# A hybrid decoder layer: a shorter chain per threshold search round, key searches over halves of 128, and the sampled u/v product moved into the front end

## What is computed

```python
z = x @ w_in                        # q, k, v, qi, ki, wi, u, vb, ga, gb
# token mixer A: a light indexer scores every visible key, each query keeps 256
sc = einsum(relu(einsum(qi, ki)), wi) * scale
_, idx = lax.top_k(sc, 256)
attn = softmax over the kept keys
# token mixer B: gMLP on chunks of 128
vn = layer_norm(vb); gm = u * (w_spatial @ vn + b_spatial)
# merge
ga, gb = sigmoid(ga + bias_a), sigmoid(gb + bias_b)
merged = ga * (attn @ w_branch_a) + gb * (gm @ w_branch_b)
h = layer_norm(alpha * x + merged @ w_o)      # then a mixture of 32 experts
```

## Time and profile before

| | us |
|---|---|
| median of 3 runs | 1486.02 (1482.46 to 1490.97) |
| the profiled execution | 1475.57 |
| its span, first to last instruction | 1474.1 |
| PE busy in the span | 1357.8 (92%) |
| DVE busy | 719.0 (49%) |
| ACT, POOL busy | 281.8, 240.7 |
| L906 (counts of the search), busy | 174.2 and 77.0 |
| `choose_keys_and_gate`, PE's first to last instruction | 291.3 to 718.4 |

### The profile page before, as it was taken

How to read it: one execution, slowest core, us unless ns; L and a number is a source line. 1 busy time by engine, 2 the same in 40 slices (tenths; PEclk the granted TensorE clock), 3 DMA queues, 4 the chain that set the end, 5 groups by cost and what they waited for, 6 DMA issues and landing times. The chain is left out here.

```text
span 1474.1 us, 19420 instructions
## 1 busy us (share of the span) xinstructions
PE 1357.8 (92%) x6779; PEld 699.5 (47%) x6779; DVE 719.0 (49%) x1687; ACT 281.8 (19%) x624; POOL 240.7 (16%) x292
## 2 busy tenths in 40 slices
PE   7999999699999999989899989899963999999986
PEld 2444444244456666656577746455541333333321
DVE  0200123488888888995365953456671111111135
ACT  0100112222231111110266420000000111111124
POOL 3121000033230000020135100001111111111103
...
GB/s 320 81 58 48 16 16 72 89 48 1 0 98 69 65 65 68 71 65 20 52 88 116 59 76 360 264 29 29 29 29 246 331 404 406 404 414 409 404 158 233
DMA packets 70330, 214.03 MB, mean 145 GB/s; under 512 B 16459, under 2 KB 42059, under 8 KB 59882
## 3 DMA queue, kind: packets, MB, share of 16 engines
...
## 5 line engine op out<-in xcount | busy, mean ns | idle before, releaser
L906 DVE TENSOR_SCALAR_CACHE_REDUCE front<-score,bound 128x384 bf16<-128x384 f32 (+2 forms) x198 | 174.2, 942 | 19.2 <-DVE bound L932 18.9
L234 PE MATMUL ps_front<-front,x_all 128*128 128x512 f32 (+1 forms) x448 | 180.4, 557 | 1.7 <-ACT wi L364 1.7
L1819 PE MATMUL main_ps_experts<-w_gate_up,main_e_rowsT 128*32 128x512 f32 (+1 forms) x1280 | 172.6, 603 | 1.6 <-DVE main_e_rowsT L1927 1.6
L234 PEld LDWEIGHTS ps_front<-front,x_all 128*128 128x128 f32 x448 | 83.2, 190 | 91.7 <-issue 81.2
L1528 PE MATMUL ps_merge<-w_o,mergedT 128*128 128x512 f32 x256 | 114.9, 608 | 3.0 <-DVE h_rows L1667 3.0
L733 PE MATMUL ps_gate<-x_all,w_gate 128*128 128x344 f32 x384 | 116.0, 461 | 0.0
L733 PE MATMUL ps_gate<-x_all,front 128*128 128x344 f32 x384 | 113.2, 453 | 0.0
L1819 PEld LDWEIGHTS main_ps_experts<-w_gate_up,main_e_rowsT 128*32 128x32 f32 (+1 forms) x1280 | 50.4, 117 | 106.6 <-issue 106.6
L1932 DVE TENSOR_TENSOR main_hidden<-main_hidden,main_ps_experts 128x256 f32<-128x256 f32 x24 | 10.1, 421 | 174.6 <-ACT main_hidden L1879 174.6
L733 PEld LDWEIGHTS ps_gate<-x_all,w_gate 128*128 128x128 f32 x384 | 74.3, 194 | 38.9 <-issue 2.4
L733 PEld LDWEIGHTS ps_gate<-x_all,front 128*128 128x128 f32 x384 | 72.7, 190 | 37.5
(11 more groups left out here) (304 smaller groups left out, 1712.5 us busy)
## 6 DMA issues: line engine op xcount, KB each, us to landing
...
w_gate_up<-pair_out SPq DMA_DIRECT2D x8, 1024.0 KB, 14.0
...
h_rows<-in_x_rows SPq DMA_DIRECT2D x9, 512.0 KB, 6.0
...
```

The costliest lines, as they stand in the source:

```text
L234: mm = nc.tensor.matmul(ps[:, g % 2, 0:c1 - c0], x_all[:, k, t * P:(t + 1) * P], w[:, k, c0:c1], start=(k == 0), stop=(k == KC - 1))
L906: V.tensor_scalar(waste[0:n, at - width:at], s, column(bound, g), None, compare, ALU.add, accum_out=column(number, g)).then_inc(taken, 1)
L1819: mm = nc.tensor.matmul(ps[c0:c1, GU, :], rowsT[j][:, k, c0:c1], w_gu[b][:, k, :], start=(k == 0), stop=(k == KC - 1))
```

## The change

- **Search.** A table of 31 powers of two (and a zero) is loaded into `bits`, the first DMA of the stage. In round r the step `other` (the bound with the next round's bit set as well, an exclusive or with column r+1 of the table) is made before the counts; after them `missed` says which rows counted too few, and `bound` becomes `other`, with the bit of column r taken back where it was missed. `found_bits`, `reached` and `bit` are gone, and with them two of the four chained steps. The two columns are addressed by the loop's register.
- **Sampled u/v product.** It moves into the front end as `make_few_uv`, four blocks of weights behind the matmuls of unit 10 and four behind those of unit 11, into bank 0. Both stages use one PSUM tensor. ACT waits for it at the end of the front end.
- **Banks for u.** u alternates between banks 6 and 0; PE waits for the copy of two tiles back. One more wait stands before tile 1 (bank 0 read) and before the first gate product in bank 6.
- **Key searches.** The one-hots are over 128 ranks, in four buffers of half the size: a place over 128 is reduced by 128 (`upper`), and the page numbers and places are split by half into four columns (`ids_by_half`, two new steps). PE does 16 matmuls with four columns per sample, ahead of single products from `at` = 3 on, and turns the places one product later.
- **Gates.** In piece 5 the products come in the order 1, 2, 0; the stores in the order merged_b, gate_a, with one more wait before gate_a in piece 5.
- **End.** The wait for the landing of the stores moves from the end of the stage to the start of `attend` on SP, POOL and DVE.

```diff
+            def make_few_uv(ks):
+                for k in ks:
+                    if k == 0:
+                        pe.wait_ge(early_in, 16 * KC // 2)
+                        pe.wait_ge(acc_read, AFTER_FEW + 5 * (NT - 1) + 4)
+                    if k >= KC // 2:
+                        pe.wait_ge(w_uv_in[k], 16)
+                    for g in range(4):
+                        mm = nc.tensor.matmul(ps[g * FEW:g * FEW + N_SAMPLE, FEW_UV_BANK, 0:QUARTER], x_few[:, k, 0:N_SAMPLE],
+                                              w_uv(k)[:, g * QUARTER:(g + 1) * QUARTER], start=(k == 0), stop=(k == KC - 1))
+                if ks[-1] == KC - 1:
+                    mm.then_inc(few_uv_full, 1)
...
             for n in range(len(units) - 2, len(units)):
                 score_dots(n)
+                make_few_uv(range(0, KC // 2) if n < len(units) - 1 else range(KC // 2, KC))
...
-        U, V, MIX, TURN = 0, 1, 2, 3
-        FEW_BANK, FEW_SQUARES, FEW, QUARTER = 4, 5, 32, GW // 2
+        ps = keep["ps_mixer"]
+        U, V, MIX, TURN = (6, FEW_UV_BANK), 1, 2, 3
...
+        def products(at):
+            return (1, 2, 0) if at == 5 else (0, 1, 2)
...
+            sp.dma_start(bits[:], ins["bits"].to_broadcast([P, 32])).then_inc(bits_in, 16)
...
-                    for which, name in ((0, "gate_a"), (1, "merged_b")):
+                    for which, name in ((1, "merged_b"), (0, "gate_a")):
+                        if at == 5 and which == 0:
+                            sp.wait_ge(gates_read, (blk - j) * 9 + at * 3 + 9)
...
-            def make_few():
-                for k in range(KC):
-                    if k >= KC // 2:
-                        pe.wait_ge(w_uv_in[k], 16)
-                    for g in range(4):
-                        mm = nc.tensor.matmul(ps[g * FEW:g * FEW + N_SAMPLE, FEW_BANK, 0:QUARTER], x_all[:, k, SEQ:SEQ + N_SAMPLE],
-                                              w_uv(k)[:, g * QUARTER:(g + 1) * QUARTER], start=(k == 0), stop=(k == KC - 1))
-                mm.then_inc(uv_full, 1)
...
             def make_uv(t):
-                for b in (U, V):
-                    if t >= 1:
-                        pe.wait_ge(uv_read, 2 * t - 1 + b)
+                if t == 1:
+                    pe.wait_ge(few_step, 4)
+                if t >= 2:
+                    pe.wait_ge(uv_read, 2 * t - 3)
+                for half, bank in enumerate((U[t % 2], V)):
+                    if half and t >= 1:
+                        pe.wait_ge(uv_read, 2 * t)
                     for k in range(KC):
-                        mm = nc.tensor.matmul(ps[:, b, :], x_all[:, k, t * P:(t + 1) * P], w_uv(k)[:, b * GW:(b + 1) * GW],
+                        mm = nc.tensor.matmul(ps[:, bank, :], x_all[:, k, t * P:(t + 1) * P], w_uv(k)[:, half * GW:(half + 1) * GW],
                                               start=(k == 0), stop=(k == KC - 1))
                     mm.then_inc(uv_full, 1)
...
                 if (at, which) == (0, 2):
                     turn(LAST - 1)
                     mix(LAST)
+                    pe.wait_ge(uv_read, 2 * NT - 2)
...
-                        for which in range(3):
+                        for which in products(at):
                             if ahead:
                                 ahead(at, which)
-                            pe.wait_ge(gates_read, i * 18 + at * 3 + which + 1)
+                            pe.wait_ge(gates_read, i * 18 + at * 3 + products((at + 4) % 6).index(which) + 1)
...
+            seek_at = {(3, 0): 0, (3, 1): 1, (3, 2): 2, (4, 0): 3, (4, 1): 4, (4, 2): 5, (5, 1): 6, (5, 2): 7}
+
+            def find_rows(at, which):
+                if (at, which) == (2, 1):
                     turn_places()
-                for b in ((), (), (0, 1), (2, 3), (4, 5), (6, 7))[at]:
+                if (at, which) in seek_at:
+                    b = seek_at[at, which]
                     pe.wait_ge(hot_ready, b + 1)
-                    for half in range(2):
-                        for g in range(PAGES):
-                            mm = nc.tensor.matmul(ps[:, TURN, b * 4 + half * 2:b * 4 + half * 2 + 2],
-                                                  hot[b % 2][:, g, half * P:(half + 1) * P],
-                                                  ids[:, b, g, :], start=(g == 0), stop=(g == PAGES - 1))
+                    for g in range(PAGES):
+                        mm = nc.tensor.matmul(ps[:, TURN, b * 4:b * 4 + 4], hot[b % HOTS][:, g, :],
+                                              ids_by_half[:, b, g, :, :].rearrange("p half c -> p (half c)"),
+                                              start=(g == 0), stop=(g == PAGES - 1))
                     mm.then_inc(hot_used, 1)
 
-            make_gates(KC // 2 - 1, between=find_rows)
+            make_gates(KC // 2 - 1, ahead=find_rows)
...
-            for tile in (bound, number, found_bits):
-                step(V.memset(tile[:], 0), wait=False)
-            step(V.memset(bit[:], 1 << 30))
+            for tile in (bound, number):
+                step(V.memset(tile[:], 0), wait=(tile is number))
             count_all(ALU.is_ge)
             step.n += N_SEARCH
             dve.wait_ge(taken, step.n)
             step(V.tensor_scalar(flip[:], number[:], float(TOPK), -1.0, ALU.is_lt, ALU.mult))
-            step(V.scalar_tensor_tensor(bound[:].bitcast(I32), found_bits[:], bit[:], flip[:],
-                                        ALU.bitwise_or, ALU.bitwise_xor))
-            per_round = N_SEARCH + 4
+            dve.wait_ge(bits_in, 16)
+            step(V.tensor_scalar(bound[:].bitcast(I32), flip[:], bits[:, 0:1], None, ALU.bitwise_xor))
+            per_round = N_SEARCH + 3
             with dve.Fori(0, 31) as r:
                 done = r * per_round + step.n
+                V.tensor_scalar(other[:], bound[:].bitcast(I32), bits[:, bass.ds(r + 1, 1)], None,
+                                ALU.bitwise_xor).then_inc(taken, 1)
                 count_all(ALU.is_ge)
-                wait_alone(dve, taken, done + N_SEARCH, idle[0])
-                V.tensor_scalar(reached[:], number[:], float(TOPK), -1.0, ALU.is_ge, ALU.mult).then_inc(taken, 1)
                 wait_alone(dve, taken, done + (N_SEARCH + 1), idle[0])
-                V.scalar_tensor_tensor(found_bits[:], reached[:], bit[:], found_bits[:],
-                                       ALU.bitwise_and, ALU.bitwise_or).then_inc(taken, 1)
+                V.tensor_scalar(missed[:], number[:], float(TOPK), -1.0, ALU.is_lt, ALU.mult).then_inc(taken, 1)
                 wait_alone(dve, taken, done + (N_SEARCH + 2), idle[0])
-                V.tensor_scalar(bit[:], bit[:], 1, None, ALU.logical_shift_right).then_inc(taken, 1)
+                V.scalar_tensor_tensor(bound[:].bitcast(I32), missed[:], bits[:, bass.ds(r, 1)], other[:],
+                                       ALU.bitwise_and, ALU.bitwise_xor).then_inc(taken, 1)
                 wait_alone(dve, taken, done + (N_SEARCH + 3), idle[0])
-                V.scalar_tensor_tensor(bound[:].bitcast(I32), found_bits[:], bit[:], flip[:],
-                                       ALU.bitwise_or, ALU.bitwise_xor).then_inc(taken, 1)
-                wait_alone(dve, taken, done + (N_SEARCH + 4), idle[0])
             step.n += 31 * per_round
...
-            step(nc.vector.tensor_copy(place[:], ps[:, MIX, 0:P].rearrange("p (g b) -> p g b", b=N_SAMPLE)))
+            turned = ps[:, MIX, 0:P].rearrange("p (g b) -> p g b", b=N_SAMPLE)
+            step(nc.vector.tensor_scalar(upper[:], turned, float(P), None, ALU.is_gt))
+            step(nc.vector.scalar_tensor_tensor(place[:], upper[:], -float(P), turned, ALU.mult, ALU.add), wait=False)
+            step(nc.vector.tensor_tensor(ids_by_half[:, :, :, 1, :], ids[:],
+                                         upper[:].rearrange("p g b -> p b g").unsqueeze(3).to_broadcast([P, N_SAMPLE, PAGES, 2]),
+                                         ALU.mult))
+            step(nc.vector.tensor_tensor(ids_by_half[:, :, :, 0, :], ids[:], ids_by_half[:, :, :, 1, :], ALU.subtract))
             step(nc.vector.tensor_copy(keep["own_taken"][:], ps[0:1, MIX, 256:256 + N_SAMPLE]))
-            dve.sem_inc(hot_used, 2)
-            with dve.Fori(0, N_SAMPLE // 2) as i:
-                for j in range(2):
-                    b = i * 2 + j
+            dve.sem_inc(hot_used, HOTS)
+            with dve.Fori(0, N_SAMPLE // HOTS) as i:
+                for j in range(HOTS):
+                    b = i * HOTS + j
                     dve.wait_ge(hot_used, b + 1)
                     for g in range(PAGES):
                         last = nc.vector.tensor_scalar(hot[j][:, g, :], rank_b[:], place[:, g, bass.ds(b, 1)], None,
                                                        ALU.is_equal)
                     last.then_inc(hot_ready, 1)
-            dve.wait_ge(hot_used, N_SAMPLE + 2)
+            dve.wait_ge(hot_used, N_SAMPLE + HOTS)
...
+        def wait_for_gates_stored(eng):
```

(6 more changed lines are left out.)

58 lines of the change are left out of this document (29 added, 29 removed).

## The result

The changed kernel takes **1466.9 us** (median of 4 runs, 1464.5 to 1468.2) against 1488.5 us for the kernel before in the same rounds. The ratio is 0.985, 95% interval 0.983 to 0.987. In two later series, on two chips, the medians were 1454.2 against 1476.5 us (ratio 0.987, 0.984 to 0.990) and 1469.1 against 1489.7 us (0.987, 0.984 to 0.990). So the change takes off 20.6 to 22.3 us in all three; on which chip the first measurement ran isn't on record. The forecast of 1462.3 us was 4.6 us too low and its range, 1455 to 1474, held the time.

What follows compares the result with a forecast made beforehand. It took the rebuilt stage as PE-bound, a faster DVE worth only PE's waits for it. A to E sum to 23.7 us: profile 1475.57 to 1451.9, median 1486.02 to 1462.3 us; range 1455 to 1474 (8 in 10).

Steps and rivals of the forecast that it cites:

- A: Front end's end: sampled product moved into PE's idle time, score matmuls faster, less a slow start; 6.0 us gained.
- B: gMLP tiles: with u in alternate banks, six PE waits for ScalarE's copy of u go; 5.0 us gained.
- C: Before the sampled positions are turned: PE's wait for DVE and the slow clock behind it vanish; 7.7 us gained.
- D: Key searches: half as many one-hot matmuls, each at a floor of some 25 ns; 3.2 us gained.
- E: Border to the next stage: PE's idle time falls from 3.95 to 2.15 us; 1.8 us gained.
- The slow start: Gate stage's start: PE idles before the border, so the gMLP product begins at half clock; 1.65 us charged.
- The search: Threshold search on DVE: two chained steps fall away; a round 0.45 us shorter, 31 rounds 14.0 us.
- the caught steps: Search rounds on DVE: small steps sometimes take 1.12 instead of 0.171 us; fewer such steps, counted at nothing.
- rival 5: Search: slower than before, each round growing as new steps are caught behind POOL instructions; 1500 us; chance 3%.
- rival 1: Search shortens too little, register-addressed operands and "other" costing more; with no gain per round 1474.8 us; chance 12%.
- the new waits of DVE, POOL and SP for the landing: Next stage's start: waits hidden behind PE's matmuls, barely; small row load 5.6 us against 6.0 us.
- the 10.5 us between profile and median: Whole kernel: the median of runs lay 10.5 us above the profiled execution; the same difference assumed after the change.

Runs made afterwards that it cites:

- few_late: Changed kernel with the sampled u/v product back at the start of the gate stage; median 1471.4 us, against 1489.4 us for the kernel before.
- one_bank: Changed kernel with one PSUM bank for u instead of two in turn; median 2.1 us above the changed kernel's, distance to attend 5.7 us more.
- whole_ranks: Changed kernel with key searches over all 256 places and two one-hot buffers; median 1471.8 us, against 1489.4 us for the kernel before.
- wait_at_end: Changed kernel with the wait for the gates' stores back at the gate stage's end; median 1468.1 us, against 1489.4 us for the kernel before.
- old_search: Changed kernel with the threshold search of before, four chained steps a round instead of two; median 8.4 us above the changed kernel's.

## Why the prediction was right

| part | predicted, us | measured, us | by |
|---|---|---|---|
| A, sampled product | 6.0 | 6.0 (5.7 by the other mark) | few_late |
| B, two banks | 5.0 | 5.7 | one_bank |
| C, hole at the turn | 7.7 | 7.6 to 8.2, not by a run of its own | see C |
| D, halves | 3.2 | 3.2 | whole_ranks |
| E, stage's end | 1.8 | 1.5 (1.8 between the two profiles) | wait_at_end |
| sum at attend's start | 23.7 | 23.9 (24.3 from the end of the unit before the last; sum of the parts 24.0 to 24.9) | profile after |

**A.** The clock in the hole stayed up as forecast (0.98 in the third stretch above) and the last scores take 1.99 us. 32 matmuls of the product take 1.91 us, where I had 1.6, but they still fit in: the scores wait for ScalarE as before, 2.12 us behind the end of the unit ahead of them in both kernels (280.75 to 282.87, and 280.36 to 282.48 before). The 1.7 us for an earlier front end came in full from that mark; only 1.3 us of it show in the start of the stage (291.32 to 290.02), because the work ahead was 0.4 us slower in this execution. The slow start cost 1.6 us, as charged.

**B.** The mis-sized term, though small: six waits cost 5.7 us and not 5.0, 1.0 each in the steady tiles and not 0.83. The tile's distance (16.06 - 15.06) holds it all; bracket plus longer refill misses 0.17 us, because the bracket counts from the end of the record ahead, and without a wait the next product starts 0.17 us before that end.

**The search.** 0.44 us per undisturbed round against 0.45 predicted. The 31 rounds together won more, 14.9 us with the front ends set equal (old_search's end at 609.2 against 594.8 us here, its stage 0.4 us earlier): on average a round is 9.33 us now ((586.2 - 306.3) / 30), 9.81 in old_search and was 9.85 us. The rest over 31 x 0.44 = 13.6 us, 1.3 us, comes from the caught steps, which I had counted at nothing: six rounds are stretched by them in old_search and in the changed kernel alike (eight in before), but they cost 8.4 us there and 7.0 us here. It doesn't matter: VectorE has the ranks ready at 643.4 (predicted 645.1), PE comes at 649.3 (649.7), so 5.9 us are spare.

**The caught steps and rival 5.** What catches them can be read from the trace. One of the changed kernel, and what GpSimd does then:

```profile
541.28 0.91 POOL L909 TENSOR_TENSOR front<-front 128x344 f32<-128x344 f32 x1 [10.66 <-ACT front L869]
541.29 0.92 DVE L943 TENSOR_SCALAR other_bound<-bound,bits 128x7 int32<-128x7 int32 x1 [0.64 <-DVE bound L949]
```

All 15 long small steps of the search in before and all 11 in the changed kernel (over 0.4 us, of 124 and 93) start while a GpSimd instruction runs and end 0.01 to 0.03 us after that instruction does. (Not every step that starts so is held: the one-column step `bit` took its 0.15 us all four times.) The share of caught steps is the same, 12%, and with fewer steps in a round less time is lost. The rival had the opposite sign: it asked for one more catch in nearly every round.

**C and rival 1.** That nothing of the hole is left, no wait and no slow clock, is in the profile. Its size is less sure. The prediction took 1.47 us off for the 17 transposes, which is their length at the slow clock; at the full clock they take 650.40 - 649.30 = 1.10 us, and without a wait PE would have gone on 0.17 us before the end of the record ahead, so the same rows give 8.2 us. By difference, what remains of the gain between main product and attend (425.1 before, 406.8 in few_late, so 18.3) after B, D and E (5.7, 3.2 and 1.8) is 7.6 us. The rival's arithmetic was that without shorter rounds PE waits 9.4 us and loses 3.1 us of clock. The run gave 9.0 and 3.2. So a rival's price was worth working out: it is what the search is worth inside the full change, 12.2 us, and more than C alone.

**D.** Right in size, and the columns are out as a price: matmuls this small, each with its weight load, cost 0.025 us each with two columns and with four.

**E.** The hole is 2.20 us (2.15 predicted); the new waits of DVE, POOL and SP for the landing are hidden, barely, as forecast: the small row that VectorE needs landed by 701.11, PE's first eight matmuls of attend end at 701.24, and the first softmax step starts at 701.33, 5.1 us after the stage's last matmul (6.0 allowed). The new order of the gates' products and stores wasn't tried apart; the 0.3 us between the two sizes of E may be its.

**From the stage to the median.** I took the 23.7 us off the span and the median alike. The measured differences are 21.6, 22.3 and 20.6 us in three series. Of the 4.6 us that the forecast was too low, 2.5 are the median of before, 1486.0 when I wrote it and 1488.5 beside the changed kernel, and 2.1 are a gain of 21.6 in place of 23.7. Two things lie between the trace and the medians. First, the recorded profile of before came from an execution without the late updates (1475.6 us), while the timed runs that I set beside it took 1482.5 to 1491.0; that those had late updates is likely and not shown, since they have no traces. Both kernels are longer by nearly the same on a chip with late updates (13 and 15 us), so that the difference nearly cancels, and the profile pair (9.2 us) was the misleading number, not the medians. The prediction took the 10.5 us between profile and median off without knowing what they were; that they cancelled was luck. Second, the stages behind attend vary by the clock that they are granted: PE was busy in the merge's first part (its products with the branch weights) for 61.8 us at a granted clock of 0.97 (wait_at_end, 67.3 us in all) and for 63.9 us at 0.94 (the profile after, 70.3 us in all, with 1.0 us more of waits). The three profiles of the changed kernel had 68.7 to 70.3 us there, where before's had 66.5 to 67.7; 2 to 3 us of the missing gain are there. Its eight variants had 66.2 to 69.7 us with the same code in that stage, so both ranges occur without a change, and chance is likely but not shown.
